# Two constant matmuls into an unread PSUM bank in each step of the first block's attention loop, ahead of that step's transposes and products

## What is computed

```python
proj = h @ w_in                       # q, k, v, indexer q/k, gates
logits = einsum('bqhd,bqkd->bhqk', q_b, kg) * attn_scale    # 8 heads, one shared k and v
logits = where(valid, logits, NEG_INF)
p = softmax(logits, -1)
attn = group_rms_norm(einsum('bhqk,bqkd->bqhd', p, vg))
mix = concatenate([attn, conv_out], -1) @ w_out
x = layer_norm(ALPHA * x + g1 * mix)
```

## Time and profile before

| | us |
|---|---|
| median of 3 runs | 1224.65 |
| lowest, highest | 1218.98, 1226.74 |
| the profiled execution, its own time | 1227.48 |
| its span, first to last instruction | 1225.7 |
| TensorE busy in the span | 1112.6 (91%) |
| mean granted TensorE clock | 0.951 |
| the attention loop, T(1) to the end of P(7) | 175.7 to 211.4 |

### The profile page before, as it was taken

One profiled execution on the slowest core, in us unless ns is written; L12 is line 12 of the kernel. 1 busy time (PEld: TensorE's weight loads), 2 busy tenths in 40 slices (PEclk: granted clock), 3 DMA queues, 4 the chain that ended last, 5 costly groups with the idle time before them and its releaser, 6 DMA issues.

```text
span 1225.7 us, 20953 instructions
## 1 busy us (share of the span) xinstructions
PE 1112.6 (91%) x8197; PEld 1024.2 (84%) x8197; DVE 760.3 (62%) x1172; ACT 574.1 (47%) x963; POOL 266.9 (22%) x257
## 2 busy tenths in 40 slices
PE   1999648999999999998999999998998799999998
PEld 1887534879999987887899999998875599999997
DVE  5747876665664446675576555567676676555554
ACT  0545334464454336542455444465455655544452
POOL 0434232013332002011123322013120023332001
PEclk9998855999999999999899999998998999999999
DMA  8654454616554625350155645563433046653650
GB/s 314 214 207 159 184 193 150 205 38 218 167 176 147 186 73 206 138 180 27 46 172 196 205 151 154 176 224 123 150 127 135 1 138 206 205 184 109 199 195 36
DMA packets 188325, 193.46 MB, mean 158 GB/s; under 512 B 13721, under 2 KB 150722, under 8 KB 188130
## 3 DMA queue, kind: packets, MB, share of 16 engines
q1 hardware_dynamic: 184016, 179.88, 43.9%
q0 software_dynamic: 2640, 10.49, 2.3%
q10 hardware_dynamic: 1602, 2.18, 0.5%
HBM read 191.48 MB, written 1.05 MB: 157 GB/s over the span
## 4 chain that ended last, share of the span: by engine, by line
PE 67%; DVE 18%; ACT 5%; DMA 4%; issue 4%; POOL 2%; ACTq 1%; POOLq 0%; SPq 0%; DVEq 0%
PE gemm L1701 20%; PE gemm L1703 19%; PE gemm L1702 19%; DVE wlo L1152 4%; DVE macc L1205 2%; DMA raw<-in_w_in 2%; ACT whi L816 2%; PE aux L2028 1%; POOL om L616 1%; DVE olo L1174 1%; PE aux L1808 1%; DVE xlo L1174 1%; DMA early<-in_w_ada 1%; DMA raw<-in_w_ada 1%; DVE om L1423 1%
## 5 line engine op out<-in xcount | busy, mean ns | idle before, releaser
L1152 DVE TENSOR_TENSOR wlo<-raw,whi 128x1024 fp32r<-128x1024 f32 (+2 forms) x348 | 399.4, 1194 | 111.8 <-ACT whi L816 111.4
L1701 PE MATMUL gemm<-ohi,whi 128*128 128x256 f32 x1536 | 437.8, 285 | 18.0 <-DVE wlo L1152 11.1
L1703 PE MATMUL gemm<-ohi,wlo 128*128 128x256 f32 x1536 | 432.6, 282 | 0.0
L1702 PE MATMUL gemm<-olo,whi 128*128 128x256 f32 x1536 | 431.8, 281 | 0.0
L816 ACT ACTIVATE whi<-raw 128x1024 fp32r<-128x1024 f32 (+2 forms) x348 | 309.3, 955 | 121.8 <-PE gemm L1703 95.5
L1701 PEld LDWEIGHTS gemm<-ohi,whi 128*128 128x128 f32 x1536 | 292.4, 190 | 28.6 <-DVE wlo L1152 15.2
L1702 PEld LDWEIGHTS gemm<-olo,whi 128*128 128x128 f32 x1536 | 292.6, 190 | 0.2
L1703 PEld LDWEIGHTS gemm<-ohi,wlo 128*128 128x128 f32 x1536 | 292.3, 190 | 0.0
L1701 PE MATMUL gemm<-acthi,whi 128*128 128x256 f32 x528 | 147.8, 280 | 0.0
L1703 PE MATMUL gemm<-acthi,wlo 128*128 128x256 f32 x528 | 147.3, 279 | 0.0
L1702 PE MATMUL gemm<-actlo,whi 128*128 128x256 f32 x528 | 147.2, 279 | 0.0
(11 more groups left out here) (310 smaller groups left out, 1529.7 us busy)
## 6 DMA issues: line engine op xcount, KB each, us to landing
raw<-in_ffn_w_in SPq DMA_DIRECT2D x44, 1024.0 KB, 6.1
raw<-in_ffn_w_out SPq DMA_DIRECT2D x32, 704.0 KB, 5.1
raw<-in_gla_w_in SPq DMA_DIRECT2D x6, 2048.0 KB, 7.6
raw<-in_diff_w_in SPq DMA_DIRECT2D x6, 2048.0 KB, 7.7
raw<-in_w_gate SPq DMA_DIRECT2D x11, 1024.0 KB, 5.2
raw<-in_w_up SPq DMA_DIRECT2D x11, 1024.0 KB, 7.5
raw<-in_w_down SPq DMA_DIRECT2D x16, 704.0 KB, 5.1
raw<-in_w_ada SPq DMA_DIRECT2D x5, 2048.0 KB, 8.1
```

The costliest lines, as they stand in the source:

```text
L1152: dve.tensor_tensor(wlo[hslot][:, q * w:(q + 1) * w], raw[slot][:, q * w:(q + 1) * w], whi[hslot][:, q * w:(q + 1) * w].bitcast(F32), ALU. ...
L1701: pe.matmul(dst, st_hi, mv_hi, start=start, stop=False)
L1702: pe.matmul(dst, st_hi, mv_lo, start=False, stop=False)
L1703: return pe.matmul(dst, st_lo, mv_hi, start=False, stop=stop_)
```

## The change

One line is added to TensorE's list. In each of the ten steps two `keep_warm` matmuls run behind the scores of the next head and ahead of the modulation sums, the transposes and the product with the values. No other engine's list and no wait of another engine is changed; no result reads the bank.

```diff
             for i in range(NH + 2):
                 if i + 1 < NH:
                     scores(i + 1)
+                keep_warm(X[2], 2)
                 for n in MOD_TAKEN.get(i, ()):
                     modulation(n)
                 if 1 <= i <= NH:
```

## The result

The changed kernel takes 1239.77 us (median of 4 runs, 1236.87 to 1241.92) against 1225.46 (4 runs): ratio 1.0126, 95% interval 1.0097 to 1.0154, so about 15 us slower. I had forecast +4.4 us, a median of 1229 and a range from 1221 to 1238. The direction was right, the size was more than three times as large, and the time lies outside the range, past the 12 us beyond which I had called it slower and given that a chance of 0.07.

A forecast was written before the change was run, and what follows sets the result against it. TensorE, with VectorE between T(2) and T(3), was taken to bound the attention loop, mostly at half clock. Terms +1.6 (i = 3) and +2.8 (i = 5 to 9) summed to +4.4 us, median 1229, range 1221 to 1238.

The forecast's parts named there:

- What bounds the kernel, and which additions lie on the path: Attention loop: additions at i = 3 and from 5 on lie on the path; those at 0, 1, 2, 4 in gaps.
- Price of one addition: Two constant matmuls, four records, on TensorE: 1.7 us at full clock, 3.4 us at half clock.
- Price of the rest at full clock: The loop's transposes, value products, scores and modulation sums on TensorE: taken to need about half their half-clock time.
- Part 1: Additions at i = 0, 1, 2, ahead of T(1): cost nothing, covered by TensorE's waits of 5.47 and 17.17 us.
- Part 2: Addition at i = 3, T(1) to T(2): +1.6 us, clock rising 4 us after it starts; bounds +0.6 to +3.4.
- Part 3: Addition at i = 4, T(2) to T(3): nothing; TensorE's 7.3 us fit within the 8.91 us VectorE needs.
- the clock that doesn't rise: Rival: the loop's clock doesn't rise at all, additions cost full half-clock price; +19.8 us, 1244.5; chance 0.07.
- Part 4: Additions at i = 5 to 9, T(3) to P(7)'s end: +2.8 us, clock rising 4 us after the first addition began.
- rises late: Rival: clock rises late or falls between additions, two more at half clock; about +8, at most +10, 1233; chance 0.15.
- Part 5: Behind the loop: nothing, since the clock is already full there.
- The rule on the clock: Claim that the skill's rule, continuous busy work brings full clock, is contradicted by the loop's trace for this mix.

The follow-up runs named there:

- four matmuls at i = 5: The changed kernel with four constant matmuls in place of two at i = 5; a single execution, 1238.35 us.
- the changed kernel with the wait on GpSimd: The changed kernel, with GpSimd's first add of slab 11 waiting until VectorE has normalised head 3; 1231.59 against 1225.33 us for the kernel before, ratio 1.0041.
- the second profile of the changed kernel: The changed kernel run once more, unaltered, beside the kernel before; 1238.14 against 1225.93 us, ratio 1.0116.
- i = 3 alone: The two constant matmuls at i = 3 only, against the kernel before: ratio 1.0049; with GpSimd also waiting for head 3's normalise: ratio 1.0028.
- a late VectorE alone: The kernel before, no constant matmul in the loop, plus two extra VectorE row maxima ahead of head 3's normalise; 1231.19 against 1225.33 us, ratio 1.0038.
- i = 5 to 9 alone: The two constant matmuls at i = 5 to 9 only, against the kernel before; 1232.53 against 1225.33 us, ratio 1.0049.
- GpSimd's adds moved: The kernel before, with GpSimd's slab 7 adds waiting for VectorE's slab 9 sum and slab 11's first add for head 3's normalise; ratio 1.0022.
- 15 constant matmuls in a row: Constant matmuls only in the two waits, 15 at i = 2 and 3 at i = 4, against the kernel before; 1230.56 against 1225.93 us, ratio 1.0051.

## Why the prediction was wrong, point by point

*What bounds the kernel, and which additions lie on the path:* right. The additions at i = 0, 1, 2 and 4 are free, those at 3 and from 5 on are paid.

*Price of one addition:* right. At half clock it took 181.34 - 177.76 = 3.58 and 205.22 - 201.65 = 3.57 us against my 3.4, but the sums right behind it came out shorter (184.61 - 181.34 = 3.27 against 3.44 us), so that net it was the 3.41 of the table. At full clock it took 219.86 - 218.04 = 1.82 against 1.7.

*Price of the rest at full clock:* the halving held. From the row with four matmuls at i = 5, a modulation sum takes 208.27 - 207.46 = 0.81 (I had 0.9), and three transposes have a duration of 0.52 against 0.88. In sum T(4) to the end took 14.8 where I had 13.8, there and in the changed kernel with the wait on GpSimd alike (223.10 - 208.27 and 214.07 - 199.25).

*Part 1 (nothing):* right. From the first group sum to T(1) it was 33.00 us after and 33.23 before, and 1.84 us of the 5.47 us of wait for slab 8 were left.

*Part 2 (+1.6):* the term was mis-sized by 1.8. It was +3.4, my own upper bound: the clock stayed at 0.50 through the addition and all behind it. In the second profile of the changed kernel it was +1.9. I had made one observed rise, 4 us after the start of the group sums, into a fixed delay. The group sums don't even bring that rise by themselves: in the two executions at i = 3 alone they are the same four records, and the clock stayed at 0.50 behind them for the whole loop (the windows of 141.50 to 219.00 above).

*Part 3 (nothing):* this step failed. I compared TensorE's 7.3 us with VectorE's 8.9 and took VectorE's 8.9 for given. It became 13.2, because the normalise of head 3 met GpSimd's add and took 4.83 us in place of 0.55. The experiments show this as the cause: a late VectorE alone brings the long stretch (13.69), and a GpSimd that waits for the normalise removes it in both kernels that had it (8.56 and 8.92). What would have shown it was in hand: VectorE's and GpSimd's timelines had 0.15 us between the end of the one and the start of the other, and the 0.59 us for which ScalarE waited for slab 11 are all that kept them in that order. I used that row only to cap a gain. The 4.3 us also take the time past every rival that I had priced except the clock that doesn't rise, and out of the range: without them the +15.1 of the trace would have been +10.8, about 1236.

*Part 4 (+2.8):* the term was mis-sized by 4.6. The step that failed is the clock's rise 4 us after the first addition of the tail began; it came after 11.7 us. Up to the first addition it was as forecast. Then the clock did not rise within slab 10's sum (1.57 us against 1.2), nor in T(4), P(3), S(7) and the next addition, which took 213.79 - 206.79 = 7.00 us where I had 3.64. The rest took 10.9 against 10.2. This is the rival "rises late", which I priced at about +8 in all, +10 at the most, and gave 0.15; its own part came out at +10.8 (3.4 + 7.4), the rest is the collision. No fixed delay would have done: with the same two matmuls at i = 5 the rise came 11.7, 11.9 (i = 5 to 9 alone), 12.4 (the changed kernel once more) and 3.0 us (with the wait on GpSimd) after they began.

*Part 5 (nothing):* right, 1013.3 against 1014.3 us.

*The rule on the clock:* after the change TensorE was busy for 15.5 us without a gap at 0.50. The sentence of the Trainium skill that the prediction cites, that an engine kept busy continuously gets the full clock (TensorE: Matmul & The Clock Gate, "Why this matters for your kernels"), fails for this mix of work here too.

*VectorE and GpSimd:* head 3's normalise took 4.83 us against 0.55, ending 0.36 us behind an add of 4.48. The Trainium skill, SBUF — State Buffer, section "Who interferes with whom", says that GpSimd and certain VectorE instructions exclude each other for a whole instruction, and that the order of issue decides which one waits. The trace agrees on the exclusion. The other order it hardly shows: slab 7's first add, which started under slab 9's products, took 5.04 us after the change (at 162.31) and 4.49 before (at 163.87). The trace agrees as well that not every VectorE instruction is held: L1347, which reads PSUM, took its 0.56 us at 198.78, inside GpSimd's add from 197.38 to 199.86. I had not applied it, because the change touches neither engine; what it touches is when VectorE comes.

*What stays open:* why the clock rises at one time and not at another in the same kernel. The changed kernel's two profiles gave 10.70 and 9.19 us for one stretch, and +15.1 and +13.6 us for the sum of the three. They don't show a rule by which one could place the matmuls. Open too is how much of the tail's price the collision brings with it.

## What to carry to other kernels

When a change shifts one engine in time, check the pairs of other engines that were apart only by chance, here VectorE and GpSimd: write down the gap and what makes it. A gap that hangs on a DMA landing late closes as soon as anything ahead of it is late. Where two engines meet like this, a wait that makes the long instruction stand back for the short one is worth a try: it cost nothing measurable in the kernel before (ratio 0.9995) and took the changed kernel from 1.0126 to 1.0041. Filling TensorE with constant matmuls was free here only in its waits, and there it gave next to nothing; on the path each pair cost its full half-clock price, 3.4 us, until the clock rose.

## What the runs showed of the hardware that I had not expected

- VectorE's normalise and GpSimd's add, released by independent paths, started within 0.01 us of each other in five profiles (after 192.82 and 192.83, at i = 3 alone 194.55 and 194.55), and each time it was VectorE that was held. In a sixth, with GpSimd's adds moved, the normalise's row starts 0.05 us ahead of the add (168.10 and 168.15) and it was held all the same (4.88 us).
- 0.9 us of added VectorE work cost 4.8 us.
- The same list on TensorE behind T(3) had its rise of the clock 15.5 us after T(3) in one execution and 6.8 us in another, which is 26.90 against 22.77 us for the tail.
- With 15 constant matmuls in a row the clock was full from 161.4 to 178.4, through 3.92 us of waiting, and it fell 1.5 us after T(1) began.
